# Tanh in place of sigmoid and SiLU in the latent attention's stretch of a two-block transformer kernel

## What is computed

```python
qk_ml = jax.nn.silu(causal_conv(qk_ml, conv_w, conv_b))      # queries and keys of the mLSTM
h_ml = mlstm_chunkwise(q_ml, k_ml, v_ml, i_gates, f_gates)   # k is scaled by 64 ** -0.5 in it
h_ml = rmsnorm(h_ml, ml_head_norm)                           # per head, with a gain
h_ml = h_ml * jax.nn.sigmoid(o_ml)                           # output gate
```

## Time and profile before

| | us |
|---|---|
| median of 3 runs | 1656.29 |
| the profiled execution | 1657.78 |
| its span, first to last instruction | 1656.0 |
| PE busy in the span | 1579.5 |
| DVE busy | 825.6 |
| ACT busy | 662.6 |
| POOL busy | 662.8 |

### The profile page before, as it was taken

One profiled execution on the slowest core, in us unless ns is written; L12 is line 12 of the kernel. 1 busy time (PEld: TensorE's weight loads), 2 busy tenths in 40 slices (PEclk: granted clock), 3 DMA queues, 4 the chain that ended last, 5 costly groups with the idle time before them and its releaser, 6 DMA issues.

```text
span 1656.0 us, 20790 instructions
## 1 busy us (share of the span) xinstructions
PE 1579.5 (95%) x7144; PEld 1285.2 (78%) x7144; DVE 825.6 (50%) x1425; ACT 662.6 (40%) x1047; POOL 662.8 (40%) x293
## 2 busy tenths in 40 slices
PE   7989999899999998999999999888998999999996
PEld 6867888777788877888888888666776788888885
DVE  5748999966684445342121244776544412112123
ACT  5544333344453445423232354446753423232331
POOL 4444444322334422444444454434215444444442
PEclk9999999999999999999999999999988999999998
DMA  5323233211232212323223232111112223223231
GB/s 194 102 77 102 91 100 100 71 59 64 101 104 101 99 55 67 105 89 102 93 98 101 89 101 89 64 46 58 39 39 77 76 89 102 94 96 101 89 101 63
DMA packets 39963, 144.43 MB, mean 87 GB/s; under 512 B 4436, under 2 KB 4564, under 8 KB 39640
## 3 DMA queue, kind: packets, MB, share of 16 engines
q1 hardware_dynamic: 38880, 139.94, 25.4%
q10 hardware_dynamic: 1016, 3.62, 0.7%
HBM read 141.43 MB, written 2.11 MB: 87 GB/s over the span
## 4 chain that ended last, share of the span: by engine, by line
PE 87%; DVE 6%; ACT 3%; issue 3%; DMA 1%; ACTq 0%; DVEq 0%; SPq 0%
PE bank L451 86%; DMA w_raw<-in_stream 1%; PE bank L560 1%; ACT w_hi L999 1%; DVE cq_rstd L1475 0%; DMA x_raw<-in_xT 0%; DVE ffy L2147 0%; PE bank L914 0%; DVE negm_diag L2012 0%; ACT a_hi L1216 0%; ACT kT L1163 0%; DVE qk_ml L1918 0%; ACT L1420 0%; DVE cn_lo L1943 0%; DVE ssq L1758 0%
## 5 line engine op out<-in xcount | busy, mean ns | idle before, releaser
L373 POOL TENSOR_TENSOR w_lo<-w_raw,w_hi 128x1024 fp32r<-128x1024 f32 x256 | 615.9, 2407 | 886.2 <-ACT w_hi L999 886.0
L999 ACT CAST w_hi<-w_raw 128x1024 fp32r<-128x1024 f32 x256 | 268.5, 1049 | 505.7 <-DMA w_raw<-in_stream 505.6
L451 PE MATMUL bank<-a_hi,w_hi 128*128 128x512 f32 x1120 | 452.9, 404 | 9.7 <-DVE a_lo L1763 6.3
L451 PE MATMUL bank<-a_hi,w_lo 128*128 128x512 f32 x1120 | 437.7, 391 | 0.0
L451 PE MATMUL bank<-a_lo,w_hi 128*128 128x512 f32 x1120 | 437.2, 390 | 0.0
L451 PEld LDWEIGHTS bank<-a_hi,w_hi 128*128 128x128 f32 x1120 | 211.1, 188 | 62.1 <-issue 13.3
L451 PEld LDWEIGHTS bank<-a_lo,w_hi 128*128 128x128 f32 x1120 | 210.9, 188 | 48.4 <-issue 4.8
L451 PEld LDWEIGHTS bank<-a_hi,w_lo 128*128 128x128 f32 x1120 | 210.6, 188 | 44.5
L451 PE MATMUL bank<-b_hi,w_hi 128*128 128x512 f32 x608 | 238.5, 392 | 0.0
L451 PE MATMUL bank<-b_hi,w_lo 128*128 128x512 f32 x608 | 236.6, 389 | 0.0
L451 PE MATMUL bank<-b_lo,w_hi 128*128 128x512 f32 x608 | 236.6, 389 | 0.0
(11 more groups left out here) (337 smaller groups left out, 1931.3 us busy)
## 6 DMA issues: line engine op xcount, KB each, us to landing
w_raw<-in_stream SPq DMA_DIRECT2D x256, 512.0 KB, 3.4
x_raw<-in_xT SPq DMA_DIRECT2D x4, 512.0 KB, 6.7
res<-in_xT ACTq DMA_DIRECT2D x1, 2048.0 KB, 7.5
out_y<-y_out SPq DMA_DIRECT2D x8, 256.0 KB, 2.0
mem_raw<-in_memT SPq DMA_DIRECT2D x1, 1024.0 KB, 12.0
mrow<-m_rows ACTq DMA_DIRECT2D x4, 256.0 KB, 3.2
consts<-in_consts SPq DMA_DIRECT2D x1, 452.0 KB, 10.1
posi<-in_positions ACTq DMA_DIRECT2D x1, 256.0 KB, 3.9
```

The lines of the kernel that those rows point to most:

```text
L373: nc.gpsimd.tensor_tensor(w_lo[:, j, :], w_raw[:, j, :], w_hi[:, j, :].bitcast(F32), ALU.subtract).then_inc(w_lo_done, 1)
L451: return nc.tensor.matmul(o, l, r, start=start, stop=stop)
L999: A.copy(w_hi[:, slot, :], w_raw[:, slot, :]).then_inc(w_hi_done, 1)
```

## The change

Each sigmoid and SiLU of the stretch becomes a hyperbolic tangent of half the argument, by sigmoid(x) = (1 + tanh(x/2)) / 2. An output gate is now two ACT instructions, the tanh and an Identity with scale and bias both gain/2, for which the column `half_gain` is made once at the start; the head norm's gain is so part of the gate, and `hml` is a product of two tiles. For queries and keys ACT writes tanh(x/2), and DVE makes (tanh + 1) * x, which is twice the SiLU, in its hooks 5 and 11. The factor of four in the scores is taken out by the constant at `sT`.

```diff
         rowinv = at("rowinv", [P, 4], small0 + 320)
         g2g = at("g2g", [P, KB], small0 + 352)
+        half_gain = at("half_gain", [P, ML_HEADS], small0 + 384)
...
+        k_tanh = at("k_tanh", [P, T], G0 + 28800)
...
             def open_gate(j):
                 act.wait_ge(evac_dve, (O["OA"] if j == 0 else O["OM"] + j - 1) + 1 - DVE_FROM)
-                A.activation(ogate[:, j, :], ogate[:, j, :], ACT.Sigmoid).then_inc(sems["o_gated"], 1)
+                half = half_gain[:, j:j + 1]
+                A.activation(ogate[:, j, :], ogate[:, j, :], ACT.Tanh, scale=0.5).then_inc(sems["o_gated"], 1)
+                act.wait_ge(sems["o_gated"], 2 * j + 1)
+                A.activation(ogate[:, j, :], ogate[:, j, :], ACT.Identity, bias=half, scale=half
+                             ).then_inc(sems["o_gated"], 1)
...
                     if j >= 2:
-                        A.activation(qk_ml[:, j, :], qk_ml[:, j, :], ACT.Silu).then_inc(sems["qk_silu"], 1)
+                        if j == 3:
+                            act.wait_ge(sems["qk_silu"], 3)
+                        A.activation(k_tanh[:, :], qk_ml[:, j, :], ACT.Tanh, scale=0.5).then_inc(sems["qk_tanh"], 1)
                         continue
...
-                        A.activation(q_ml[2 * j + e][r, :], qk_ml[r, j, :], ACT.Silu).then_inc(sems["qk_silu"], 1)
+                        A.activation(q_ml[2 * j + e][r, :], qk_ml[r, j, :], ACT.Tanh, scale=0.5
+                                     ).then_inc(sems["qk_tanh"], 1)
...
                             ).then_inc(sems["gains_ready"], 1)
+            V.tensor_scalar(half_gain[:, :], col("ml_head_norm_2", 0, ML_HEADS), 0.5, None, ALU.mult
                             ).then_inc(sems["gains_ready"], 1)
...
-                    V.scalar_tensor_tensor(out=sT[:, u % 2, w], in0=ps[3][:, w], scalar=float(ML_QK) ** -0.5,
+                    V.scalar_tensor_tensor(out=sT[:, u % 2, w], in0=ps[3][:, w], scalar=0.25 * float(ML_QK) ** -0.5,
...
-                    dve.wait_ge(sems["o_gated"], h + 1)
+                    dve.wait_ge(sems["o_gated"], 2 * h + 2)
...
-                    V.scalar_tensor_tensor(out=hm, in0=ps[0][:, :], scalar=col("ml_head_norm_2", h),
-                                           in1=ogate[:, h, :], op0=ALU.mult, op1=ALU.mult).then_inc(sems["ml_gated"], 1)
+                    V.tensor_tensor(hm, ps[0][:, :], ogate[:, h, :], ALU.mult).then_inc(sems["ml_gated"], 1)
+
+            def twice_silu(pair, out, x, t, n):
+                dve.wait_ge(sems["qk_tanh"], 3 * pair + n + 1)
+                V.scalar_tensor_tensor(out=out, in0=t, scalar=1.0, in1=x, op0=ALU.add, op1=ALU.mult
+                                       ).then_inc(sems["qk_silu"], 1)
 
             def ml_hook(n):
+                if n - 1 in SILU_AT:
+                    j = SILU_AT[n - 1][0]
+                    for e in range(2):
+                        r = slice(ML_QK * e, ML_QK * e + ML_QK)
+                        q = q_ml[2 * j + e][r, :]
+                        twice_silu(j, q, qk_ml[r, j, :], q, e)
+                    k = qk_ml[:, j + 2, :]
+                    twice_silu(j, k, k, k_tanh[:, :], 2)
                 for h in range(ML_HEADS):
```

More of the change, by code:

```diff
@@ L122 @@
 squares_added ssq_added ssqg_added start_hi start_ready start_scaled stat_ready stat_root tap_done topk_done
-topk_step uq_out vm_rows wi_copied wi_turned x2_done x2_gained y_pool y_scaled y_written
+topk_step uq_out vm_rows wi_copied wi_turned x2_done x2_gained y_pool y_scaled y_written qk_tanh
 """
@@ L1280, in _ @@
             act.wait_ge(sems["pv_done"], 4 * MLA_G)
+            act.wait_ge(sems["gains_ready"], 2)
             act.dma_start(posi[:, :], pos_in.to_broadcast([P, T])).then_inc(sems["late_landed"], 16)
@@ L1542, in _ @@
             V.tensor_tensor(g2g[:, :], col("norm_final_g", 0, KB), col("norm_pre_mix_2", 0, KB), ALU.mult
+                            ).then_inc(sems["gains_ready"], 1)
+            V.tensor_scalar(half_gain[:, :], col("ml_head_norm_2", 0, ML_HEADS), 0.5, None, ALU.mult
                             ).then_inc(sems["gains_ready"], 1)
@@ L1875, in rotary @@
                                     ).then_inc(sems["rope_step"], 1)
-            dve.wait_ge(sems["gains_ready"], 1)
+            dve.wait_ge(sems["gains_ready"], 2)
             feed_forward("FF1", 0, res, last_ff1, rotary)
```

## The result

The changed kernel takes 1657.81 us, the median of 20 runs (1654.01 to 1659.97), against 1655.20 for the kernel before (20 runs, 1652.89 to 1659.18). The ratio is 1.0014, 95% interval 1.0008 to 1.0021: slower by 2.3 us (1.3 to 3.5). That is a real difference but lies within the 0.2% that the prediction counts as no change. The two profiled executions have the same span, 1656.0 us, but the one of after comes 3 us earlier to the stretch, on work that the change doesn't touch, so the stretch is to be read by itself.

What follows compares the result with a forecast made beforehand. PE bounds the kernel, busy 1579.5 of 1656.0 us, so only its idle or lower-clock time pays. Terms -0.55 + 0.1 + 6.2 + 2.3 - 0.45 - 0.25 - 3.2 = +4.15 on 1656.3 give 1660.4 us, range 1651 to 1665.5.

Steps and rivals of the forecast that it cites:

- rival 2: Stall comes, but only 1 us lost to clock after it and 4 us gained at the end: 1656.4 us, chance 0.15.
- start: Ahead of the first exponents: tanh, Identity and rounding take 2.33 us instead of 2.88, PE gains 0.55 us.
- unit 5: Pair 0's DVE instructions meet POOL multiplications; DVE's idle time just covers it: 0.1 us lost, up to 1.5.
- stall in unit 11: Pair 1's DVE instructions wait for POOL, putting off negm_diag and o_rows: PE loses 6.2 us, bounds 2.1 and 7.5.
- lower clock behind it: After 8.6 us of PE idle in unit 11, 4.6 us at half speed: 2.3 us lost, bounds 1 and 3.5.
- hook 16: Behind this gate, without its table load, mix_lo and PE's next values come 0.45 us earlier.
- hook 22: At this gate ACT is behind by less, PE idle 0.58 us: a gain of 0.25 us.
- hook 28 in the stretch: Last gate: decay and PE 1.95 us sooner without two loads, plus 1.25 us of clock; together 3.2 us gained.
- the last term of the sum: Less lower clock from 1216.5 to the first output matrix products: a third of 4 us, 1.25, bounds 0 and 4.
- Rival 1: POOL does not hold DVE back for long, so stall and clock losses go: 1651.9 us, faster, chance 0.20.
- Rivals 3 and 4: Both pairs hurt, 1665.5 us, chance 0.11; or tanh needs its own table set, switches stay, 1664.9 us, chance 0.04.
- rival 3: Units 5 and 11 both hurt, end at lower clock, longer slow spell behind the stall (+1.0): 1665.5 us, chance 0.11.

Runs made afterwards that it cites:

- the two fastest: Changed kernel with pair 1's DVE instructions later and POOL's multiplications first, 0.9941; gates alone by tanh with POOL's multiplications first, 0.9945; both against the kernel before.
- the kernel with both remedies: Changed kernel with pair 1's three DVE instructions at hooks 14, 16, 17 and POOL's six multiplications ahead of its subtractions: ratio 0.9941 to the kernel before.

## Why the prediction was right, and where its sizes were off

It gave 1660.4 us within 1651 to 1665.5; measured is 1657.81. Direction and cause were right. The most probable answer, slower by over 0.2%, was not: 0.14% is within the bound, which had 0.32 against 0.48. The sum said +4.15 us, the measurement +2.3, about halfway to the +0.1 of rival 2. Of the 2.6 us between 1660.4 and 1657.81, 1.1 come from the start value, 1656.29 us of three runs where 20 give 1655.20. By its steps:

| step | predicted | measured in the traces |
|---|---|---|
| start | -0.55 | -0.3 (PE's wait 5.82 to 5.53); -0.5 in five kernels with the same start (5.31 to 5.32) |
| unit 5 | +0.1 | +0.03 (PE idle 1.56, then 1.59) |
| stall in unit 11 | +6.2 | +6.1 (2.42, then 8.49) |
| lower clock behind it | +2.3 | +3.35 |
| hook 16 | -0.45 | -0.75 |
| hook 22 | -0.25 | 0 |
| hook 28 in the stretch | -3.2 | -4.5 (from 1200.74 to the first product of the output matrix 22.84 us, then from 1205.67 18.35 us) |
| clock behind the stretch | none | -1.4 (3.36, then 1.93) |
| sum | +4.15 | +2.5 |

The steps within the stretch give +3.9 where its windows differ by 3.44, so 0.5 us of gain is not in the table. Most of it lies between PE's waits of hooks 16 and 22: from 1175.54 to 1200.74 are 25.20 us in before, from 1180.99 to 1205.67 are 24.68 us in after, and the table has only 0.18 of that. The sum of +2.5 agrees with the +2.3 by the ratio.

**Where it was right.** The stall was worked out as seven POOL instructions in place of four, plus 0.45 us for each long DVE instruction that holds POOL up. Both are in the rows of after (one multiplication 1.74 us, where two took 2.62; one subtraction 2.79 against 2.38). The Identity took 0.81 us as worked out from two column costs.

**The step that failed** is the last term of the sum, the clock at the end. The prediction saw that the rows didn't say how much of it would go, and took a third of 4 us. The lower clock didn't come at all there. From the last `sT` product to the first product of the output matrix before takes 6.53 us (1217.05 to 1223.58) and after 4.03 (1219.99 to 1224.02): 2.5 us. Another 1.4 us came from the 3.2 us beyond the stretch that before ran at the lower clock, for which the sum had nothing. Together 3.9 us where 1.25 was taken: the mis-sized term, as the runs with the last gate and with the gates alone showed. The prediction's upper bound of 4 us matches this by luck: it was meant for the 6.53 us alone, and half speed in these can cost 3.3 us at most. Half of rival 2, the clock that "goes well", came true at this end.

**The clock behind the stall** was too small by 1.05 us: 6.7 us at half speed and not 4.6. The value was stretched from the 3.6 us seen behind a wait of 5.82 us. This error and that of the last term have opposite signs, so that the whole came out nearer than its parts is luck in part.

**Start and hooks.** At the start the exponent came 0.44 us nearer to the gate and not 0.55: the rounding and the exponent behind it don't overlap by a tenth, as their starts are 1.04 us apart before the load and 1.05 in after. PE's wait at hook 22 didn't shrink: it is 0.58 us in both.

```profile
1205.67 0.41 PE L453 MATMUL bank<-v_mla,probsT 128*128 128x64 f32 x2 [0.58 <-DVE mix_lo L2124]
```

At hook 16 it fell from 1.77 to 1.20, and a piece of 0.18 us behind it went too.

```profile
1180.99 0.41 PE L453 MATMUL bank<-v_mla,probsT 128*128 128x64 f32 x2 [1.20 <-DVE mix_lo L2124]
```

**The rivals.** Rival 1, no blocking, was wrong in its strongest form: even an instruction of two columns waits. Rivals 3 and 4 did not occur. The clock behind the stall was longer, as rival 3 had it, but pair 0 was not hurt and the end was free.

## What to carry to other kernels

Count a table load only where the consumer ends up waiting for it: here 2 of 19 were worth all that could be measured, since they also kept TensorE from its lower clock. A DVE instruction with both inputs in SBUF can take as long as what POOL is running, so before moving work from ACT to DVE, look at POOL's row in the same microseconds and at what stands behind in DVE's list; a place with an idle POOL made the same work free here, and an input in PSUM kept a small one from waiting. When a change measures as nothing, time its halves: here -7 and +8 us looked almost like no change.

## What the runs showed of the hardware that was not expected

- A 128x2 instruction on DVE took 1.2 us in place of 0.16 with both inputs in SBUF beside a busy POOL.
- Who goes first, DVE or POOL, can hang on 0.01 us: `negm_diag` took 0.28 us when it started 0.02 us ahead of POOL, and 1.44 and 2.55 us when it started 0.01 and 0.02 us ahead. So the lead in the profile doesn't tell the winner, and unit 11 came out one POOL instruction longer where it was lost. That one kernel's time varies in this way between executions is likely but not shown.
- A longer wait isn't always a loss. The kernel with only its last gate changed waited 3.66 us for `o_rows` in unit 11, not 2.42, though DVE and POOL took the same time there: 11.00 us from the start of POOL's row of instructions to `o_rows` in both. PE came sooner. In before it had run at the lower clock behind its waits of 1.60 us (1137.91) and 2.50 us (1147.02); in this kernel it had the same two waits and kept the full clock, and stood longer instead. The two rows are of before, then the one of the kernel with its last gate changed:

```profile
1137.91:1141.40 3.49, 3.49 (x11) 2.92 (x12) 1.35 (x4) 0.59 (x1) 0.00 (x0) 0.51 0.00 0
1148.10:1151.60 3.50, 3.50 (x16) 2.90 (x14) 3.36 (x8) 3.42 (x6) 3.50 (x3) 0.51 0.01 2
```
```profile
1134.00:1152.00 18.00, 10.08 (x58) 8.00 (x59) 13.40 (x33) 13.93 (x28) 11.41 (x7) 1.00 0.18 61
```

- The granted clock at the end follows the idle pieces, but not by them alone. All five kernels with PE's long idle pieces (0.84 and 1.76 us) run at the lower clock there. Seven have the short ones (the changed one and six others). In five of these the full clock holds on into the output matrix; in the two fastest it falls just before that begins:

```profile
1217.40:1220.40 3.00, 3.00 (x10) 2.37 (x8) 1.56 (x9) 2.08 (x3) 0.00 (x0) 0.53 0.00 0
```

This is a window of the kernel with both remedies. It costs 1.3 us, and what decides it stays open.
